# One inference step with a mixture of experts on one core: position table by factors and loads by halves at the head, another order, slot-space scaling and sums in PSUM on the residual at the tail

## What is computed

```python
xp = layer_norm(x_prompt, ln_in_g, ln_in_b)                      # 128 context tokens
xs = layer_norm(x_sample + pos_embed_2d(256, 1024), ln_in_g, ln_in_b)   # 256 latent tokens
# pos_embed_2d: row r and column c of the 64-wide grid, [sin(r f), cos(r f), sin(c f), cos(c f)]
h = x * (1.0 + sc1) + sh1                                        # from silu(c) @ w_ada + b_ada
u = h @ p['w_in']                                                # convolution + two scans | FNet mixing
x = layer_norm(ALPHA * x + g1 * mix, p['ln1_g'], p['ln1_b'])
h2 = x * (1.0 + sc2) + sh2
# hierarchical MoE: top-1 of 4 groups, top-2 of its 4 experts, comb[t, e] the weight
hid = jax.nn.silu(t @ w_gate[e]) * (t @ w_up[e]) * comb[..., None]
y2 = sum over e of hid @ w_down[e]
x = layer_norm(ALPHA * x + g2 * y2, p['ln2_g'], p['ln2_b'])
```

## Time and profile before

| what | value |
|---|---|
| median of 3 runs | 502.61 us (501.02 to 505.34) |
| the profiled execution | 503.42 us, of which its span, first to last instruction, is 501.4 us |
| mean granted TensorE clock | 0.962 of 2.4 GHz |
| PE busy | 439.5 us (88%) |
| DVE busy | 240.5 us (48%) |
| ACT, POOL busy | 120.8 us (24%), 56.0 us (11%) |
| moved by DMA | 147.16 MB, 293 GB/s over the span |

### The profile page before, as it was taken

One profiled execution on the slowest core, in us unless ns is written; L12 is line 12 of the kernel. 1 busy time (PEld: TensorE's weight loads), 2 busy tenths in 40 slices (PEclk: granted clock), 3 DMA queues, 4 the chain that ended last, 5 costly groups with the idle time before them and its releaser, 6 DMA issues.

```text
span 501.4 us, 6442 instructions
## 1 busy us (share of the span) xinstructions
PE 439.5 (88%) x2370; PEld 239.4 (48%) x2370; DVE 240.5 (48%) x439; ACT 120.8 (24%) x242; POOL 56.0 (11%) x58
## 2 busy tenths in 40 slices
PE   0777999999999998899999999999999998898500
PEld 0343555556554465794554355544445544553200
DVE  2651623847734257920122343444444444246797
ACT  2300158783220226251120111111111111220100
POOL 2000015357540340000000000000000000000000
PEclk9989899999999999899999999999999999999855
DMA  8999992855999045804999999999999999996003
GB/s 317 387 386 340 341 387 78 291 213 202 353 326 338 5 156 207 308 3 151 331 396 395 356 369 395 396 394 390 392 396 395 392 391 395 394 396 251 1 1 125
DMA packets 65011, 147.16 MB, mean 293 GB/s; under 512 B 3576, under 2 KB 4408, under 8 KB 64968
## 3 DMA queue, kind: packets, MB, share of 16 engines
q1 hardware_dynamic: 63776, 143.66, 77.7%
q10 hardware_dynamic: 1032, 2.81, 1.6%
q0 software_dynamic: 160, 0.10, 0.2%
HBM read 144.99 MB, written 1.58 MB: 292 GB/s over the span
## 4 chain that ended last, share of the span: by engine, by line
PE 77%; DVE 11%; DMA 5%; issue 4%; ACT 2%; SPq 0%; ACTq 0%; DVEq 0%
PE PS L1664 18%; PE PS L1432 12%; PE PS L1702 9%; PE PS L1533 8%; PE PS L1670 5%; PE PS L1363 4%; PE PS L1737 4%; DMA ring<-in_ex_w_gate 4%; PE PS L1608 4%; PE PS L1415 2%; PE PS L1709 1%; PE PS L1466 1%; PE PS L1744 1%; DMA rowB<-in_colsB 1%; PE PS L1684 1%
## 5 line engine op out<-in xcount | busy, mean ns | idle before, releaser
L1664 PE MATMUL PS<-ring,xs 128*64 128x256 f32 x896 | 102.9, 382 | 2.2 <-DMA ring<-in_ex_w_gate 1.7
L1664 PEld LDWEIGHTS PS<-ring,xs 128*64 128x64 f32 x896 | 61.9, 137 | 38.6 <-issue 10.1
L1432 PE MATMUL PS<-hT,ring 128*128 128x388 f32 x192 | 68.7, 511 | 3.9 <-DVE hT L849 3.9
L1702 PE MATMUL PS<-ring,hTs 128*64 128x512 f32 x224 | 52.9, 615 | 1.5 <-DMA ring<-in_ex_w_down 1.0
L1170 DVE SCALAR_TENSOR_TENSOR y<-PS,comb,y 128x1024 f32<-128x1024 f32 x42 | 53.5, 1278 | 0.3 <-PE PS L1744 0.3
L1432 PEld LDWEIGHTS PS<-hT,ring 128*128 128x128 f32 x192 | 37.7, 199 | 33.0 <-issue 7.7
L694 ACT CAST yh<-PS 128x512 fp32r<-128x512 f32 x14 | 8.2, 585 | 98.5 <-PE PS L1702 58.6
L1156 DVE TENSOR_TENSOR yl<-PS,yh 128x512 fp32r<-128x512 f32 x14 | 9.7, 691 | 44.6 <-ACT yh L694 44.6
L1702 PEld LDWEIGHTS PS<-ring,hTs 128*64 128x64 f32 x224 | 15.2, 140 | 31.8 <-issue 31.7
L1363 PE MATMUL PS<-ring,cond 128*32 128x512 f32 x192 | 24.9, 635 | 0.0
L1737 PE MATMUL PS<-yh,selT 64*128 64x512 f32 x84 | 20.8, 490 | 4.5 <-DVE y L1170 2.6
(11 more groups left out here) (256 smaller groups left out, 569.6 us busy)
## 6 DMA issues: line engine op xcount, KB each, us to landing
ring<-in_ex_w_gate SPq DMA_DIRECT2D x16, 2048.0 KB, 13.5
ring<-in_ex_w_up SPq DMA_DIRECT2D x16, 2048.0 KB, 15.9
ring<-in_ex_w_down SPq DMA_DIRECT2D x16, 2048.0 KB, 14.8
ring<-in_w_ada SPq DMA_DIRECT2D x12, 2048.0 KB, 14.4
ring<-in_w_in SPq DMA_DIRECT2D x3, 2048.0 KB, 20.5
ring<-in_w_out SPq DMA_DIRECT2D x2, 2048.0 KB, 10.4
xn<-in_x_sample SPq DMA_DIRECT2D x2, 512.0 KB, 6.3
pos<-in_pos SPq DMA_DIRECT2D x2, 512.0 KB, 7.2
```

The lines of the kernel that those rows point to most:

```text
L1432: mm = pe.matmul(PS[:, w % 4, 0:W], wt[:, k, (w % 4) * P:(w % 4 + 1) * P], hT[:, k, :], start=(k == 0), stop=(k == KD - 1))
L1664: mm = pe.matmul(PS[HALF * h:HALF * (h + 1), j, 0:FE // 2], x(k, HALF), w[:, k, h * (FE // 2):(h + 1) * (FE // 2)], start=(k == 0), stop=( ...
L1702: mm = pe.matmul(PS[HALF * h:HALF * (h + 1), 3, :], x, w[:, f, h * 512:(h + 1) * 512], start=(f == 0), stop=(f == KF - 1))
```

## The change

At the head the position table becomes one of 64 rows of [sin, cos] of n times the frequencies: the column half is the same for each latent tile and is loaded once, the row half is one table row, broadcast over 64 partitions. SP issues nine loads there instead of five, six of them of 64 partitions and 128 KB. DVE starts with the statistics of tile 0; the copy to `cols` goes between statistics and root of tile 1, silu between those of tile 2; ACT's exponentials follow its root of tile 1. PE waits for the condition only before `ada_sums(0)`. Units 1 and 2 are loaded in halves with a semaphore for each. `ada_sums(3)` moves ahead of `project(3)`, which is split around `ada_cols(GB)`.

At the tail down of expert 14 is loaded, and used, ahead of gate and up of expert 15. The banks in PSUM are assigned anew so that all three results of expert 14 are out before expert 15's down product. For expert 15 the weights go from token space to slot space: `slot_marks` on DVE (during expert 11) and `slot_weights` on PE give each slot its comb, DVE makes the row comb times g2 for each slot (`slot_gates`), and one multiplication (`scale_last`) scales the down product. `rest(i)` puts the residual tile ALPHA x + g2 y into PSUM with a product with the identity, `combine_last(i)` adds the scaled output there in float32, and the normalisation reads PSUM (`rest_var`, `spread`). Tile 0's residual is made by POOL. The last tile is finished and stored in two halves.

```diff
-    r = np.repeat(np.arange(LAT // GRID_W, dtype=np.float32), GRID_W)[:, None] * freqs[None]
-    k = np.tile(np.arange(GRID_W, dtype=np.float32), LAT // GRID_W)[:, None] * freqs[None]
-    pos = np.concatenate([np.sin(r), np.cos(r), np.sin(k), np.cos(k)], axis=-1).astype(np.float32)
+    k = np.arange(GRID_W, dtype=np.float32)[:, None] * freqs[None]
+    pos = np.concatenate([np.sin(k), np.cos(k)], axis=-1).astype(np.float32)
...
-                if i > 0:
-                    sp.dma_start(pos[:, i - 1, :], t["pos"][(i - 1) * P:i * P]).then_inc(pos_in[i - 1], 16)
+                for h in range(2):
+                    src = t["pos"][2 * (i - 1) + h].partition_broadcast(HALF) if i else t["pos"]
+                    sp.dma_start(pos[HALF * h:HALF * (h + 1), i, :], src).then_inc(pos_in[i], 16)
...
+                if u in half_in:
+                    k0 = KD // 2
+                    sp.dma_start(dst[:, 0:k0, :], src[:, 0:k0, c0:c0 + 512]).then_inc(half_in[u], 16)
+                sp.dma_start(dst[:, k0:, :], src[:, k0:, c0:c0 + 512]).then_inc(ring_in[(u + 1) % RING], 16)
...
             if j < 2:
-                return j if e == 0 else 3 * e - 1 + j
-            return min(3 * e + 4, NU - 1)
+                return j if e == 0 else 3 * e - 1 + j + (e == LAST)
+            return min(3 * e + 4, NU - 1) if e != LAST - 1 else 3 * LAST - 1
...
-            for w in range(4):
+            for w in range(3):
                 project(w, range(KD // 2))
-                if w == 1:
-                    ada_sums(2)
-            ada_sums(3)
+                if w:
+                    ada_sums(w + 1)
+            project(3, range(KD // 4))
             ada_cols(GB)
+            project(3, range(KD // 4, KD // 2))
...
-                b = c_banks(e, i)
-                src = PS[:, b:b + 2, :].rearrange("p a n -> p (a n)")
+                src, y = both(c_banks(e, i)), halves(y12[:, i, :])
...
+            link(pool.tensor_scalar(xn[:, 0, :], xn[:, 0, :], ALPHA, None, ALU.mult))
+            pool.wait_ge(s["g2_sb"], 4)
+            pool.wait_ge(s["acc_done"], NT * (LAST - 1) + 1)
+            link(pool.tensor_tensor(y12[:, 0, :], y12[:, 0, :], g2r[:, 0, :], ALU.mult))
+            pool.tensor_tensor(y12[:, 0, :], y12[:, 0, :], xn[:, 0, :], ALU.add).then_inc(s["pool_settled"], 1)
...
+            choose(LAST - 1)
+            gather(LAST - 2, 0)
+            slot_copy()
+            gather(LAST - 2, 1)
+            slot_gates()
+            y_low(LAST - 1)
+            gather(LAST - 2, 2)
+            choose(LAST)
+            silu(LAST)
             gather(LAST - 1, 0)
-            settle(0)
-            y_low(LAST)
             gather(LAST - 1, 1)
+            hidden(LAST)
             gather(LAST - 1, 2)
+            dve.wait_ge(s["x1_done"], NT)
             settle(1)
             settle(2)
-            most = most_of(dve)
-            for i in range(NT):
-                gather_z(LAST, i)
...
+            scale_last()
...
+            turn(LAST - 1)
+            combine(LAST - 2, 0)
+            slot_weights()
+            combine(LAST - 2, 1)
+            project_out(LAST - 1)
+            combine(LAST - 2, 2)
+            pe.wait_ge(s["ab_sb"], 1)
+            project_in(LAST, 0)
+            combine(LAST - 1, 0)
+            combine(LAST - 1, 1)
+            project_in(LAST, 1)
+            combine(LAST - 1, 2)
             turn(LAST)
-            combine(LAST - 1, 0)
-            most = most_of(pe)
+            rest(0)
             project_out(LAST)
-            combine(LAST - 1, 1)
-            combine(LAST - 1, 2)
             for i in range(NT):
-                combine(LAST, i)
+                if i:
+                    rest(i)
+                combine_last(i)
```

More of the change, by code:

```diff
@@ L349, in most_of, with overflow @@
             return eng.value_load(cnt[0:1, 0:1], min_val=0, max_val=TOK)
-        def overflow(eng, most, body):
+        def overflow(eng, most, body, before=None, after=None):
             with eng.If(most > CAP):
+                if before:
+                    before()
                 with eng.Fori(1, PASSES) as pb:
@@ L1195, in _ @@
             hidden(0)
-            for e in range(LAST):
+            for e in range(LAST - 1):
                 silu(e + 1)
@@ L1760, in _ @@
             project_in(0, 1)
-            for e in range(LAST):
+            most = most_of(pe)
+            for e in range(LAST - 1):
                 project_in(e + 1, 0)
```

331 lines of the change are left out of this document (226 added, 105 removed).

## The result

The changed kernel takes 488.92 us (median of 4 executions, 486.53 to 491.81) beside 502.78 us of the kernel before on the same chip: ratio 0.973, interval 0.970 to 0.977. The direction was right; the time lies 5.9 us above the forecast and 0.4 us above the upper end of the range. The kernel was run twice more during the study (486.76 and 488.96 us); all fifteen executions lie between 486.01 and 491.81 us, with a median of 488.3.

A forecast was written before the change was run, and what follows sets the result against it. Expert phase taken as one stream of loads, started by the first unit PE frees, with only DVE working at the end. Profiled 503.42 less 5.6 (head) and 14.0 (tail) gives 483.8; median 0.8 lower: 483.0 us, range 479.5 to 488.5.

The forecast's parts named there:

- DVE's start at the head: Head: DVE starts at 4.8 us instead of 10.68, so `ada_sums(0)` starts at 16.4; 2.9 us gained, bounds 2.4 and 3.4.
- Tile 1 takes 4.2 ... 12.3: Head, on DVE: tile 1 takes 4.2 us, copy and split add perhaps 0.3, so it is done at 12.3 us.
- The loads: ... is 0.7 us less: Head: position loads shrink from 1,048 to 786 KB, 0.7 us less at 394 GB/s.
- No row of before has such a load of whole rows: Head rival, chance 0.25: position loads writing 64 partitions run at half rate; the head gives 1 to 2 us less, 484.3 us.
- The second modulation: Head, around `ada_cols`: 2.0 us gained by the new order, 0.8 by PE's clock, bounds 0 and 1.7.
- Nothing else in between changes: Between head and tail: PE is the limit and loads follow its freed slots, so the head's 5.6 us carries through.
- The tail up to the gate product: Tail: expert 15's gate product ends at 456.8 us in the old clock, with 1.3 us taken for `slot_weights`.
- POOL: Tail: POOL multiplies and adds tile 0 in 2.68 + 2.35 us until 464.2; PE stands 1.4 us before `rest(0)`.
- 1.76: 466.0: Tail: `rest(0)`, two full products on PE, takes 1.76 us and ends at 466.0 us.
- the second rival: Tail, chance 0.18: PE's clock falls at its wait before `rest(0)`; down 1.8 us more, `rest(0)` 0.9, `combine_last` up to 0.9; 486.6 us.
- From down to the statistics: Tail: `scale_last` with hand-over until 470.4 us, then `combine_last(0)` in 0.9, so statistics start at 471.4 us.
- the first two rivals: Slow position loads at the head (0.25, 484.3 us) and PE's clock falling at the tail (0.18, 486.6 us); together 487.9.

The follow-up runs named there:

- pos128_plain: The changed kernel with the position table expanded in HBM and brought by three loads of 128 partitions instead of six of 64; 485.02 us, ratio 0.963.
- pos64_plain: The changed kernel with the position table expanded in HBM, still six loads of 64 partitions but no broadcast source; 488.24 us, ratio 0.970.
- tail_only: The kernel before with only the change's tail edits, its head left as it was; 492.21 us, ratio 0.980.
- head_only: The kernel before with only the change's head edits, its tail left as it was; 500.29 us, ratio 0.995.

## Why the prediction missed

Both parts gain where the prediction said. What failed were the rate taken for the position loads and the sizes of several steps of the tail, `rest(0)` above all. The three profiled executions of the changed kernel have a mean of 488.6 us where the sum had 483.8. Of these 4.8 us, 2.1 are missing at the last `g2_row` (441.32 on average, 3.5 sooner than before instead of 5.6) and 3.2 from there to the statistics; behind them 0.4 come back. The forecast also set the median 0.8 below the profiled execution; here it is 0.3 below (488.3). Point by point, in the order of the prediction's steps:

- **DVE's start at the head**: 4.78 and 7.77 us came as said. "Tile 1 takes 4.2 ... 12.3" failed: it assumed the factors to be there. `ada_sums(0)` started at 18.47 instead of 16.4. With loads that reach all partitions at full rate it starts at 16.48 (pos128_plain), and the first restart is 2.51 us sooner than before, inside the bounds of 2.4 to 3.4 that stood around 2.9. So this term was right but for the loads.
- **"The loads: ... is 0.7 us less"** is the step that failed at the head. Fewer bytes took more time: 242 to 300 GB/s from 4 to 12 us, 263 in the first profile, where the kernel before moved 392. The mechanism stood among the rivals with 0.25 ("No row of before has such a load of whole rows"), at a price of 1 to 2 us; it costs about 2. What the trace of before could not show is now there: the stretch moves 266 GB/s with halves, 353 with every second partition, 397 with all.
- **The second modulation**: 2.0 for the order is right (2.0 and 2.1); 0.8 for the clock is 1.7. Of the 0.9 us more, the wait of 1.19 us for `dft` left nothing in the first profile.
- **"Nothing else in between changes"** left out that PE's clock at the dispatch differs from execution to execution. In the profiled execution this cost 1.4 us; over the seven profiles with the change's head the 24 products take 6.0 us on average, 5.8 and 6.0 in the two with the old head. So it explains the profiled execution, not the median.
- **The tail up to the gate product**: forecast 456.8 in the clock of before, measured 456.07 + 1.41 = 457.5. The 0.7 us are PE's waits of 0.84 and 0.53 us around `slot_weights`, which the sum didn't have; the tiny products themselves took 0.65 where 1.3 was taken.
- **POOL** ended 7.45 us behind the gate product (forecast 7.4), and PE waited 1.35 (1.4): right, with some luck. POOL's first step started 2.66 us behind the gate product instead of 2.3 and took 2.36 us instead of 2.68.
- **`rest(0)` "1.76: 466.0"** is the most mis-sized term of the tail: 3.4 to 3.7 us in four of the eight profiles with the wait, all three of the changed kernel among them, and 1.98 in the others. This was the second rival (0.18), whose argument against itself, that the wait is 1.4 us here and not 3.6, does not hold. Its price was shared out wrongly, though: it had 1.8 us for down, 0.9 for `rest(0)` and up to 0.9 for `combine_last`. Measured were 1.4 to 1.7 for `rest(0)`, 0 to 0.3 for down (3.65, 3.84 and 3.91), and nothing for `combine_last` (1.13, as everywhere).
- **From down to the statistics** 1.8 us were taken. pos64_plain, where the clock stayed, needs 2.5: `combine_last` 1.06 instead of 0.9, and some 0.3 us at the hand-over from PE to DVE and again from DVE to PE. With 0.1 to 0.2 more for `rest(0)` at full clock this makes 15.5 instead of 14.6.

The tail's account: 14.2 - 0.7 - 0.9 = 12.6, which tail_only's profile shows (12.55 sooner), less up to 1.7 for the clock. The causes of the first two rivals came true at once; "together 487.9" stood in the text, and the median of all executions is 488.3. That these two numbers are so close is partly luck: the second rival's 3.6 us stood for 1.7 of clock, and the rest of the miss at the tail came from terms that no rival had. They had been given little weight each, and the likeliest case took the better side of both. What stays open is the last us or two of the head by the medians (the seven profiles with its whole head are on average 3.8 us sooner at the last `g2_row`, head_only's median says 2.7, with 1.1 to 4.1 as interval), and what decides in one execution whether the clock falls at the dispatch, at down of expert 14, or at `rest(0)`: the runs show that it varies with the same instructions and the same waits, not why.

## What to carry to other kernels

Load to all partitions at once, or to every second one, but not to one half: here a table cut to three quarters of its bytes cost 2 us. Expanded in HBM, so that three plain loads of 128 partitions bring the same 786 KB, it gave them back. Where PE must wait for a slower engine just ahead of the last products, put work that is ready in front of the waiting step: together with a reordered DVE step it gave 3.2 us where the wait itself was 1.35, since behind the wait `rest(0)` ran at the lower clock in four of eight profiles. When several small risks point the same way, the likeliest total is not the sum of each one's best case; and one profile of a kernel whose PE has short waits is one draw of its clock.
